# Cached value pages loaded from ScalarE's queue, one step behind the sums, instead of from SyncE's

## What is computed

```python
past_k = cache_k[l][page_table].reshape(n_dec, past_len, A_HEADS, A_HD)
past_v = cache_v[l][page_table].reshape(n_dec, past_len, A_HEADS, A_HD)
...
s = jnp.einsum('nqhmd,nkhmd->nhmqk', q, k).astype(jnp.float32) * (A_DH ** -0.5)
p = jax.nn.softmax(jnp.where(mask, s, -jnp.inf), axis=-1)
p = p[:, :, 0] - lam * p[:, :, 1]
return jnp.einsum('nhqk,nkhe->nqhe', p.astype(v.dtype), v)
```

## Time and profile before

| what | value |
|---|---|
| median of 3 runs | 1558.6 us (1558.01 to 1558.85) |
| the profiled execution | 1560.54 us, its span 1558.8 us |
| PE busy | 1349.5 us, 87% of the span |
| PEld busy | 841.4 us, 54% |
| DVE busy | 764.7 us, 49% |
| ACT busy | 298.9 us, 19% |
| POOL busy | 293.5 us, 19% |
| granted TensorE clock, mean | 0.932 |
| DMA | 284.41 MB, mean 182 GB/s over the span |

### The profile page before, as it was taken

How to read it: one execution, slowest core, us unless ns; L and a number is a source line. 1 busy time by engine, 2 the same in 40 slices (tenths; PEclk the granted TensorE clock), 3 DMA queues, 4 the chain that set the end, 5 groups by cost and what they waited for, 6 DMA issues and landing times.

```text
span 1558.8 us, 21435 instructions
## 1 busy us (share of the span) xinstructions
PE 1349.5 (87%) x7166; PEld 841.4 (54%) x7166; DVE 764.7 (49%) x1413; ACT 298.9 (19%) x924; POOL 293.5 (19%) x215
## 2 busy tenths in 40 slices
PE   7899989979889997896686886687989988988998
PEld 4444865645555554464454553354657767765443
DVE  2565126787787886774465294354211142452001
ACT  2212123324434333223123100000000100000000
POOL 1222102132131134220111121232000021340010
PEclk9899999999999998998878987889999997999999
DMA  6510214447657646758999967777574752545231
GB/s 211 181 67 35 105 47 134 150 152 221 216 161 223 217 149 194 220 174 271 291 306 333 264 217 211 241 246 237 168 231 127 231 180 87 174 159 196 81 122 68
DMA packets 274509, 284.41 MB, mean 182 GB/s; under 512 B 29521, under 2 KB 205590, under 8 KB 273750
## 3 DMA queue, kind: packets, MB, share of 16 engines
q1 hardware_dynamic: 257534, 247.06, 51.8%
q10 hardware_dynamic: 16864, 35.97, 6.1%
HBM read 235.56 MB, written 47.52 MB: 182 GB/s over the span
## 4 chain that ended last, share of the span: by engine, by line
PE 51%; DVE 14%; SPq 11%; issue 10%; DMA 8%; POOL 3%; ACT 3%; ACTq 0%; POOLq 0%; DVEq 0%
PE ps L1643 14%; PE ps L1908 7%; PE ps L1596 6%; PE ps L1661 6%; DMA sa<-in_cache_v 4%; PE ps L1606 4%; PE ps L1775 3%; SPq L428 3%; SPq L426 3%; PE ps L1722 3%; DVE tr L1207 2%; PE ps L1690 2%; DVE sm L1345 2%; SPq L421 2%; DVE sa L1282 1%
## 5 line engine op out<-in xcount | busy, mean ns | idle before, releaser
L1643 PE MATMUL ps<-hT,r 128*128 128x344 f32 x1728 | 590.9, 485 | 8.6 <-ACT tr L915 4.0
L1643 PEld LDWEIGHTS ps<-hT,r 128*128 128x128 f32 x1728 | 328.5, 202 | 183.8 <-issue 56.8
L720 POOL TENSOR_TENSOR sa<-sa 128x512 f32<-128x512 f32 x128 | 180.3, 1414 | 550.6 <-DVE sa L1284 253.9
L1690 PE MATMUL ps<-sa 128*2 128x129 f32 x2048 | 88.6, 288 | 72.8 <-DMA sa<-in_cache_v 72.2
L1282 DVE TENSOR_TENSOR sa<-sa 128x512 f32<-128x512 f32 x128 | 97.2, 759 | 56.1 <-DMA sa<-in_cache_k 55.9
L1596 PE MATMUL ps<-r,hT 128*128 128x512 f32 x256 | 116.9, 611 | 0.0
L1690 PEld LDWEIGHTS ps<-sa 128*2 128x2 f32 x2048 | 39.2, 84 | 134.5 <-DMA sa<-in_cache_v 99.6
L1908 PE MATMUL ps<-r,hT 128*128 128x512 f32 x256 | 110.3, 592 | 0.0
L1284 DVE TENSOR_REDUCE sa<-sa 128x8 f32<-128x512 f32 x128 | 86.8, 678 | 25.6 <-POOL sa L720 25.6
L924 ACT ACTIVATE tr<-ps 128x344 f32<-128x344 f32 x48 | 22.0, 459 | 366.8 <-PE ps L1643 359.2
L1775 PE MATMUL ps<-r 128*128 128x128 f32 x512 | 72.9, 296 | 19.8 <-DMA r<-kv_dram 15.9
(11 more groups left out here) (273 smaller groups left out, 1451.9 us busy)
## 6 DMA issues: line engine op xcount, KB each, us to landing
sa<-in_cache_k SPq DMA_DIRECT2D x256, 256.0 KB, 3.1
sa<-in_cache_v SPq DMA_DIRECT2D x256, 256.0 KB, 3.6
r<-in_w_f SPq DMA_DIRECT2D x36, 512.0 KB, 5.5
r<-in_w_up SPq DMA_DIRECT2D x24, 512.0 KB, 3.7
r<-kv_dram SPq DMA_DIRECT2D x40, 256.0 KB, 5.0
g_dram<-tr ACTq DMA_DIRECT2D x16, 516.0 KB, 4.5
tr<-g_dram SPq DMA_DIRECT2D x24, 344.0 KB, 4.4
cv_dram<-tr ACTq DMA_DIRECT2D x12, 512.0 KB, 4.4
```

The costliest lines, as they stand in the source:

```text
L720: nc.gpsimd.tensor_tensor(prod[:, 2 * (gp % 2), :], kring[:, 2 * (gp % 3), :], qB[:, j % 2, :], ALU.mult).then_inc(s["even_mul"], 1)
L1643: ins = nc.tensor.matmul(ps[:, b, 0:G3], wf[f % 4][:, k * P:(k + 1) * P], hT[:, k, cg * G3:(cg + 1) * G3], start=(k == 0), stop=(k == KD - 1))
L1690: ins = nc.tensor.matmul(ps[32 * h:32 * h + 2, 7, 0:HD + 1], pr[:, p, 2 * h:2 * h + 2], vring[:, v % RV, h, :], start=(p == 0), stop=False ...
```

## The change

`load_v` moves from SP's program to ACT's. SP no longer fills the ring at the start and no longer reloads value slots. ACT fills all six slots at its first cached step, at the start of order A. In step i it then loads into the slots that the sums of step i-1 emptied (`summed(j, i - 1)`, and the last step of the round before for i = 0), before with a wait for `v_used` of the page, as on SP. The slots, their number and the semaphores stay as they were.

```diff
+    def summed(j, i):
+        return [(j - 1) * NPAGE + p for p in pv_pages(i)] if j >= 1 else []
...
@@ in the program of SyncE
-        def load_v(v):
-            vp = sp.value_load(ptab[0:1, ds(v, 1)], min_val=0, max_val=a["cache_v"].shape[1] - 1)
-            src = a["cache_v"][0, ds(vp, 1)].rearrange("o p h d -> (o p) h d")
-            sp.dma_start(vring[:, v % RV, :, 0:HD], src).then_inc(s[f"vin{v % RV}"], 16)
...
-        for v in range(RV):
-            load_v(v)
...
-                    if j >= 1:
-                        for p in pv_pages(i):
-                            v = (j - 1) * NPAGE + p
-                            if v + RV < NS * NPAGE:
-                                sp.wait_ge(s["v_used"], v + 1)
-                                load_v(v + RV)
@@ in the program of ScalarE
+        def load_v(v):
+            vp = act.value_load(ptab[0:1, ds(v, 1)], min_val=0, max_val=a["cache_v"].shape[1] - 1)
+            src = a["cache_v"][0, ds(vp, 1)].rearrange("o p h d -> (o p) h d")
+            act.dma_start(vring[:, v % RV, :, 0:HD], src).then_inc(s[f"vin{v % RV}"], 16)
...
+                    if (j, i) == (0, 0):
+                        act.wait_ge(s["ptab_in"], 16)
+                        act.wait_ge(once("ring_ones"), nth("ring_ones"))
+                        for v in range(RV):
+                            load_v(v)
+                    for v in summed(j, i - 1) if i else summed(j - 1, SA_STEPS - 1):
+                        if v + RV < NS * NPAGE:
+                            act.wait_ge(s["v_used"], v + 1)
+                            load_v(v + RV)
                     yield
```

## The result

The changed kernel takes 1581.1 us in the median of 4 runs (1572.9 to 1586.7) against 1558.3 before: a ratio of 1.0144, with a 95% interval of 1.0096 to 1.0192. It is slower, as forecast (1570 us), by twice the forecast 11 us. The profiled execution is its fastest, 1572.9 us, so the traces account for 12.4 of the 23 us; what the slower executions do in addition no profile of this kernel shows.

The account below looks back on a forecast made before the run. SP's issue bounds order 3, DMA engines order 1; PE, DVE and ACT bound each other in order A. Terms 25 + 12 - 1 + 0 - 26 + 2 = +12 on 1560.5 profiled gave 1572.5, median forecast 1570 us; range 1520 to 1608.

Parts of the forecast that it names:

- the ring's filling: Start of order A: six first loads, 8 us of ACT's queue, mostly covered; +2 us.
- the slots: Order A: slots refilled late because ACT reaches its loads late, 0.7 us in each of 36 active steps; +25 us.
- ACT's late results: Order A: three loads hold ACT's queue for 4.0 us, delaying copies that PE waits for; +12 us.
- a term for it in order 3: 941 to 1175 us: PE's granted clock rises from 0.89 to 0.93 with fewer gaps; -8 us.
- 12 of the 36 steps cost 2 us each, half of which isn't felt: Order A: how the delay of ACT's own results behind its loads was sized; 12 us.
- Orders 1 and 2, forecast -1: 696 to 870 us: -1, since the DMA engines bring loads no sooner; 870 to 941 us: 0.
- Order 3, forecast -26: 941 to 1175 us: fewer PE waits for values -25, clock -8, longer landings some +7; together -26 us.
- what I took back for late slots: 941 to 1175 us: ACT's loads late by some 1 us every second or third step; 15 of 40.1 us idle.
- The signs I had named: Order A: value waits over 15 us, 8 us a step; order 3: waits below 20, step about 5.3, clock above 0.89.
- ACT's idle time covers it: Rival: order A costs 12 us together, 941 to 1175 us gives -43; 1523 us in all; chance 0.36.
- ACT saturates: Rival: in order A more than half of each load burst lies on PE's path, 75 us; 1608 total; chance 0.15.
- The DMA engines take it back: Rival: in 941 to 1175 us landings lengthen, giving only -12 against 12 in order A; 1558.6 us; chance 0.09.

Follow-up runs that it names:

- e10: Kernel before, but in order A only ACT issues the value loads, in the same step as the sums; 1585.3 us against 1555.7, ratio 1.019.
- e3: Kernel before, plus small dummy loads that nobody reads, issued on ACT where the changed kernel loads values; 1581.8 us against 1560.9, ratio 1.0145.
- e8: Kernel before, but value loads on ACT one step behind the sums in orders 1 to 3, SP in order A; 1549.8 us against 1555.9.
- e7: Kernel before, but value loads on ACT one step behind the sums in order A only; 1593.8 us against 1555.9, ratio 1.0229.
- e5: Kernel before, but value loads on ACT in the same step as the sums in order 3 only; 1524.0 us against 1555.9, ratio 0.9796.
- e4: Kernel before, but value loads on ACT one step behind the sums in order 3 only; 1545.9 us against 1560.9, ratio 0.9923.
- e6: Kernel before, but value loads on ACT in the same step as the sums in orders 1 to 3, SP in order A; 1518.9 us against 1555.9.
- e1: Kernel before, with value loads still on SP but one step behind the sums throughout; 1630.3 us against 1560.9, ratio 1.043.

## Why the prediction came out as it did

The direction and its mechanism were right: a loss in order A above a gain in order 3. The measured 1581 lies in the range and 11 us above the 1570 that I gave, so that the loss is twice the forecast one. For the profiled execution I had 1572.5, and it took 1572.9. That is luck: against the forecast, order A came out 2 us shorter, orders 1 and 2 8.7 shorter, order 3 13.1 longer and the rest 2.1 shorter, and errors within order A cancelled too. Point by point:

*Order A, forecast +39 with the ring's filling, measured +37.0.* The sum came out and its parts were wrong. I gave the slots 25 us and ACT's late results 12, all of it idle time of PE, and the clock nothing, though I had a term for it in order 3. The windows show 23.2 us of idle time and 13.8 of busy time at a granted clock of 0.94 for 0.96. So 37 us of idle time were forecast and 23 came, and the clock term that I had left out made up for it.

The experiments show that the parts were the wrong way round, too. Issue from ACT without any late slot costs 29.7 us in order A (e10), or 18.7 with the cheaper loads of e3, and the step behind adds 7 to 15. The step of the working that was mis-sized is "12 of the 36 steps cost 2 us each, half of which isn't felt". The feature copy and the transposes' copy alone took 20.4 and 12.1 us in e10 where they took 6.9 and 3.2 before; the absence of slack at the feature banks was named, and its weight was not. The slots' waits rose by 21.3 - 2.9 = 18.4 us, 0.5 a step where I took 0.7, but that idle time stands partly in place of ACT's, so it can't be added to e10's: taking the step behind away gives back less than its waits by the medians (8.3), since ACT's late results then show in their place.

*Orders 1 and 2, forecast -1, measured -9.7.* For the change by itself the forecast was right (e8: -0.9). What I had left out is that these stretches make up some of a delay: 6 us come back there in e7 and e10. In the traces PE's wait for the chunks from tab_dram shrinks, 23.5 us before, 18.1 in e7, 21.2 in e10 and 11.2 in the changed kernel; what makes it shrink was not tested.

*Order 3, forecast -26, measured -12.9.* The step that failed is what I took back for late slots, 15 of the 40.1 us: PE's waits for values came down to 31.8 us only. I had them late by 1 us "at every second or third step"; the size was right and the number was not, with 30 such waits, 1.1 us each, in 33 active steps. Landings were 4.2 us in the median for 3.5, and the clock rose by 0.01 (0.89 to 0.90, or 0.91 to 0.92 from round 6 on) where I had counted 0.04. The step behind costs 16 us in this stretch (e5 against e4, 255.0 and 270.8 us from round 6 to the up-projection). Without it, the stretch gains 28.7 us: the 26 that I forecast is about what the move of issue is worth without the step behind.

*The signs I had named.* In order A they came: waits for value pages over 15 us, more waits for 906 and 966, and 8.2 us a step in round 2, (552.7 - 471.2)/10. In order 3 two of three failed: the waits are 31.8 us and not below 20, a step of round 6 takes (1035.6 - 978.1)/10 = 5.8 us and not 5.3, and the clock is just above 0.89.

*The rivals.* "ACT's idle time covers it" fell in order A (e10, e3) and holds in order 3. "ACT saturates" did not come: order A lost 37 us, 44 in e7, and not 75. "The DMA engines take it back": landings do lengthen, to 6.2 us in e5 at 259 GB/s, and the stretch is still 29 us shorter, so they took little of it. By the rule of the Trainium skill ("DMA: Bandwidth & Descriptors", section "Issuing engines are not separate DMA queues") a second issuer only saves time of issuing. The runs agree: in order 3, where SP's issue was short of time, it gave 29 us in the same step (e5); in orders 1 and 2, at a DMA share of 0.88 before, it gave 5 to 10 in the same step (e6) and under 1 a step behind (e8).

*What stays open.* The median is 8 us above the profiled execution. In e7, whose lists in order A are those of the changed kernel, order A takes 725.9 us and not 718.6, so a part of it can be lost there; that it is was not shown.

## What to carry to other kernels

Moving DMA issue to another engine is two changes, the queue that pays for issuing and the moment at which a slot is refilled, and they are to be priced apart and by stretch. An engine that is idle for two thirds of its time can still have no room in its queue, if its results are what the bottleneck waits for (order A); with 6% of work it had room for all the value loads (order 3). Don't refill a ring a step late when it only has two steps of depth: here that cost about 8 us in order A from ACT, 16 in order 3 and 67 in order A from SP, and refilling at once from the queue that is free in each stretch made the kernel 2.4% faster than it had been. When a forecast adds idle time to a stretch, ask what it does to the clock there: in order A PE's busy time was 14 of the 37 us.

## What the runs showed of the hardware beyond what I had expected

A DMA issue with its register load takes about as long on ACT as on SP, 1.27 and 1.33 us. In order A the value loads from ACT's queue land in 4.4 us in the median (4.2 in e10), where those from SP's took 3.5 (also in e1, where they were a step late), though fewer bytes moved per second (168 and 171 GB/s against 179). Key and value loads now go out side by side instead of one after the other; that this is the cause is argued, not tested. PE's granted clock went with its gaps: 0.91 with 40 us of them in 224, 0.95 with 25 in 195. By these means 224 x 0.09 = 20 us of full-speed time weren't granted before and 195 x 0.05 = 10 in e5, so that some 10 of the 14 us of busy time saved are the clock's, beside 15 of gaps (an estimate). In order A it went the other way, 0.96 with 51 us of gaps in 466 and 0.94 with 74 in 503.
